# A one-core decoder layer on Trainium2: residual rows moved into the first two expert rounds, empty rounds moved to the front of the loop

## The reference

```python
x  = LayerNorm(ALPHA * x + g1 * mix)
u2 = x * (1 + sc2) + sh2
x  = LayerNorm(ALPHA * x + g2 * HierMoE(u2))   # top-1 group, then top-2 experts in that group
```

## Time and profile before

| | us |
|---|---|
| median of 3 runs | 1728.73 (1726.45 to 1728.82) |
| profiled execution, its own time | 1728.13 |
| its span, first to last instruction | 1726.0 |
| PE busy | 1568.4 (91%) |
| DVE busy | 532.8 (31%) |
| ACT busy | 203.7 (12%) |
| POOL busy | 88.4 (5%) |
| mean granted TensorE clock | 0.963 of full |

### The profile page before, as it was taken

The page is one execution under the profiler, slowest core; times in us unless marked ns, Lnnn a source line. Parts: engine busy times, 40 slices in busy tenths (PEclk is TensorE's granted clock), DMA queues, the critical chain, the costliest instruction groups (busy, mean ns, idle before and its releaser), DMA issues.

```text
span 1726.0 us, 24825 instructions
## 1 busy us (share of the span) xinstructions
PE 1568.4 (91%) x9617; PEld 896.4 (52%) x9617; DVE 532.8 (31%) x948; ACT 203.7 (12%) x343; POOL 88.4 (5%) x174
## 2 busy tenths in 40 slices
PE   3799999999999998999977999999989889899893
PEld 0256666535777754577745444444435444344351
DVE  0110029611322324422164332323223232232325
ACT  0000010200000013320043000000000000100002
POOL 3000000000111100010001000000000000000000
PEclk8799999999999899899987999999999999999997
DMA  9999988875444363454336999999999999999991
GB/s 362 422 416 400 370 316 318 324 292 209 158 135 153 132 221 121 172 207 153 137 152 243 361 419 409 415 425 424 414 400 418 399 417 415 406 424 419 418 386 61
DMA packets 79394, 537.01 MB, mean 311 GB/s; under 512 B 10385, under 2 KB 10561, under 8 KB 18065
## 3 DMA queue, kind: packets, MB, share of 16 engines
q1 hardware_dynamic: 72146, 507.62, 73.5%
q0 software_dynamic: 6576, 26.35, 4.5%
q10 hardware_dynamic: 624, 2.36, 0.3%
HBM read 533.40 MB, written 11.80 MB: 316 GB/s over the span
## 4 chain that ended last, share of the span: by engine, by line
PE 71%; DMA 17%; DVE 5%; SPq 3%; ACT 2%; issue 2%; ACTq 0%; DVEq 0%
PE ps L616 15%; PE ps L1165 14%; DMA ring<-w_gate 12%; PE ps L1008 7%; PE ps L1190 6%; PE ps L629 6%; PE ps L600 4%; PE ps L1147 3%; SPq L407 3%; DMA ring<-w_ada 3%; DMA arena<-w_in 2%; PE ps L686 2%; PE ps L662 1%; PE ps L1117 1%; DVE arena L2037 1%
## 5 line engine op out<-in xcount | busy, mean ns | idle before, releaser
L1165 PE MATMUL ps<-ring,arena 128*64 128x256 f32 x3200 | 358.8, 383 | 21.2 <-DMA ring<-w_gate 20.0
L1165 PEld LDWEIGHTS ps<-ring,arena 128*64 128x64 f32 x3200 | 227.6, 138 | 167.8 <-DMA ring<-w_gate 33.3
L616 PE MATMUL ps<-arena,ring 128*128 128x288 f32 x1024 | 256.9, 409 | 0.0
L616 PEld LDWEIGHTS ps<-arena,ring 128*128 128x128 f32 x1024 | 191.9, 190 | 69.7 <-issue 18.4
L1190 PE MATMUL ps<-arena 128*64 128x512 f32 x800 | 181.5, 601 | 20.2 <-DVE arena L2055 12.9
L600 PE MATMUL ps<-ring,silu_c 128*32 128x512 f32 x768 | 103.7, 658 | 38.0 <-POOLq L513 19.4
L1008 PE MATMUL ps<-arena,ring 128*128 128x288 f32 x512 | 124.7, 406 | 0.0
L1190 PEld LDWEIGHTS ps<-arena 128*64 128x64 f32 x800 | 54.5, 138 | 131.2 <-issue 93.0
L629 PE MATMUL ps<-ring,arena 128*128 128x512 f32 x256 | 117.0, 605 | 1.3 <-ACT arena L1263 0.7
L1147 PE MATMUL ps<-arena 64*128 64x512 f32 x384 | 104.5, 636 | 12.3 <-DVE arena L2037 10.7
L1008 PEld LDWEIGHTS ps<-arena,ring 128*128 128x128 f32 x512 | 97.2, 190 | 26.8
(11 more groups left out here) (451 smaller groups left out, 1263.0 us busy)
## 6 DMA issues: line engine op xcount, KB each, us to landing
ring<-w_gate SPq DMA_DIRECT2D x100, 1024.0 KB, 23.5
ring<-w_up SPq DMA_DIRECT2D x100, 1024.0 KB, 25.8
arena<-w_down SPq DMA_DIRECT2D x100, 1024.0 KB, 26.4
ring<-w_ada SPq DMA_DIRECT2D x96, 1024.0 KB, 10.6
ring<-w_in SPq DMA_DIRECT2D x52, 1024.0 KB, 6.5
ring<-w_o SPq DMA_DIRECT2D x16, 1024.0 KB, 6.3
ring<-cache_k SPq DMA_DIRECT2D x16, 512.0 KB, 4.4
ring<-cache_v SPq DMA_DIRECT2D x16, 512.0 KB, 4.3
```

Of the source, the lines that this page charges most:

```text
L616: last = mm(ps[:, bank, 0:T], ring[:, slot, P * t:P * (t + 1)], uT[:, t, :], start=(t == 0), stop=(t == KC - 1))
L1165: last = mm(ps[B * s:B * (s + 1), 2 + c // 4, 0:256], xgT[:, 4 * (c % 4) + t, :], ring[:, c, 512 * t + 256 * s:512 * t + 256 * (s + 1)], s ...
```

## The change

Five edits.

1. The calls 12 to 23 of `turn_tokens` are gone from ahead of the loop. Instead PE has `turn_x1` and DVE `x1_rows`: at the end of round 0 the tiles 0 and 2 (eight pieces), at the end of round 1 the tile 1 (four pieces). They go piece by piece through two PSUM banks. PE ends each of these two rounds by waiting for DVE's last piece. `acc` is zeroed by two POOL memsets first, and ALPHA times x is added to it.
2. The loops count so that empty rounds come first: `If(n + nblocks >= NBLK)`, with `i` computed in the body. PE's `turn_rows(1)` is now inside the loop.
3. The rank product stands before calls 10 and 11 of `turn_tokens`; the product for the lists follows at once, `idxs` comes before `plan`, and the experts' numbers are counted across partitions and turned by a small PE product.
4. `ln2b` is loaded by SP behind the last expert's weights, not by POOL ahead of the loop.
5. `gain_sample(0)` stands ahead of `centre(1)`; some buffers have other addresses.

```diff
@@ SP
-            with sp.Fori(1, NBLK) as i:
-                with sp.If(i < nblocks):
+            with sp.Fori(1, NBLK) as n:
+                with sp.If(n + nblocks > NBLK):
+                    i = nc.s_assert_within(sp.snap((n + nblocks + (64 - NBLK)) % 64), 0, NBLK - 1,
...
+            sp.wait_ge(tt_pe, 24)
+            sp.dma_start(ln2b, ln2.partition_broadcast(P)).then_inc(ln2_loaded, 16)
@@ POOL
             link(g.memset(xg, 0.0))
+            g.memset(acc[0], 0.0)
+            g.memset(acc[1], 0.0).then_inc(acc_clear, 1)
...
-            pool.wait_ge(tt_pe, 24)
-            pool.dma_start(ln2b, ln2.partition_broadcast(P)).then_inc(late_loaded, 16)
@@ PE
             for n in range(1, 12):
+                if n == 10:
+                    pe.wait_ge(rt_dve, 1)
...
                 turn_tokens(n, u2T)
...
-            for n in range(12, 24):
-                if n < 16:
-                    pe.wait_ge(x1_act, 4 * (n - 12) + 4)
...
-            turn_rows(1)
+            def turn_x1(first, i):
+                t0, tn = TILES[i]
+                for q in range(4):
+                    x = first + q
+                    if x >= 2:
+                        pe.wait_ge(xr_dve, x - 1)
+                    for m in range(4):
+                        last = nc.tensor.transpose(ps[0:tn, (4, 7)[x % 2], P * m:P * (m + 1)],
+                                                   rT[:, 4 * q + m, t0:t0 + tn], ident[:])
+                    last.then_inc(tt_pe, 1)
...
-            with pe.Fori(0, NBLK) as i:
-                with pe.If(i < nblocks):
+            with pe.Fori(0, NBLK) as n:
+                with pe.If(n + nblocks >= NBLK):
...
+                    with pe.If(i < 1):
+                        turn_rows(1)
...
+                    with pe.If(i < 1):
+                        pe.wait_ge(x1_act, KC)
+                        turn_x1(0, 0)
+                        turn_x1(4, 2)
+                        pe.wait_ge(xr_dve, 8)
+                    with pe.If(i > 0):
+                        with pe.If(i < 2):
+                            turn_x1(8, 1)
+                            pe.wait_ge(xr_dve, 12)
@@ DVE
+            gain_sample(0)
             for q in range(1, 4):
                 centre(q)
                 scale_rows(q)
-                gain_sample(q - 1)
-            gain_sample(3)
+                gain_sample(q)
...
-            link(v.tensor_tensor(ecmp, bc(cum[0:1, :], 1, NB1), bc(iotab[0:1, 0:NB1], 2, NE), ALU.is_le))
+            link(v.tensor_scalar(ecmp, cum, tokid[:, 0:1], None, ALU.is_le))
...
+            def x1_rows(first, i):
+                for q in range(4):
+                    x = first + q
+                    dve.wait_ge(tt_pe, 13 + x)
...
+                        v.tensor_scalar(xsrow.rearrange("t (p m) -> t m p", m=KC)[:, 4 * q:4 * q + 4, :], src,
+                                        ALPHA, None, ALU.mult).then_inc(xr_dve, 1)
...
+                        v.scalar_tensor_tensor(w, src, ALPHA, w, ALU.mult, ALU.add).then_inc(xr_dve, 1)
...
-            with dve.Fori(0, NBLK) as i:
-                with dve.If(i < nblocks):
+            with dve.Fori(0, NBLK) as n:
+                with dve.If(n + nblocks >= NBLK):
...
-            dve.wait_ge(late_loaded, 5 * 16)
+            dve.wait_ge(late_loaded, 4 * 16)
+            dve.wait_ge(ln2_loaded, 16)
```

More of the change, by code:

```diff
@@ L180, in layer @@
         xg = area(16384, D, parts=B)
[L181 to L184, removed]
+        xgT = area(18432, KC, B)
+        hid = area(19456, 256)
+        hsil = area(19712, 256)
+        hT = area(19968, 2, P)
         yout = area(13312, 1024)
@@ L580, in _ @@
                                ln2[:, 512 * q:512 * (q + 1)].partition_broadcast(32)).then_inc(late_loaded, 16)
-            with pool.Fori(0, NBLK) as i:
-                with pool.If(i < nblocks):
+            with pool.Fori(0, NBLK) as n:
+                with pool.If(n + nblocks >= NBLK):
+                    i = nc.s_assert_within(pool.snap((n + nblocks + (64 - NBLK)) % 64), 0, NBLK - 1,
+                                           skip_runtime_bounds_check_because="the branch holds it there")
                     pool.wait_ge(gathered, i * 16 + 16)
@@ L1084, in _ @@
             for n in range(1, 12):
-                turn_tokens(n, u2T)
[L1087 to L1093, removed]
-            last.then_inc(rt_pe, 1)
-            for n in range(12, 24):
-                if n < 16:
-                    pe.wait_ge(x1_act, 4 * (n - 12) + 4)
[L1098 to L1105, removed]
+                if n == 10:
+                    pe.wait_ge(rt_dve, 1)
+                    for i in range(3):
+                        mm(ps[:, 2, NE * i:NE * (i + 1)], causal[:, 0:P], both[:, i, :], start=True, stop=(i == 0))
+                        for k in range(i):
+                            mm(ps[:, 2, NE * i:NE * (i + 1)], ones[:], both[:, k, :], start=False, stop=(k == i - 1))
+                    for i in range(3):
+                        last = mm(ps[:, 3, 0:NE], ones[:], both[:, i, :], start=(i == 0), stop=(i == 2))
+                    last.then_inc(rt_pe, 1)
+                turn_tokens(n, u2T)
+            pe.wait_ge(rt_dve, 2)
+            for k in range(2):
+                for i in range(3):
+                    last = mm(ps[0:B, 4, 0:NB1], rsel[k][:, i, :], bsel[k][:, i, :],
+                              start=(k == 0 and i == 0), stop=(k == 1 and i == 2))
+            last.then_inc(rt_pe, 1)
+            pe.wait_ge(rt_dve, 3)
+            mm(ps[0:1, 5, 0:NB1], eid[0:NB1, :], ident[0:NB1, 0:NB1], start=True, stop=True).then_inc(rt_pe, 1)
             pe.sem_inc(moe_used, MOE_CHUNKS - SLOTS)
@@ L1433, in _ @@
                   ).then_inc(x1_act, 1)
[L1434 to L1441, removed]
             for nn in range(2):
@@ L1453, in _ @@
             copy_rows(1)
-            with act.Fori(0, NBLK) as i:
-                with act.If(i < nblocks):
+            with act.Fori(0, NBLK) as n:
+                with act.If(n + nblocks >= NBLK):
+                    i = nc.s_assert_within(act.snap((n + nblocks + (64 - NBLK)) % 64), 0, NBLK - 1,
+                                           skip_runtime_bounds_check_because="the branch holds it there")
                     act.wait_ge(moe_used, i * MOE_CHUNKS + (MOE_CHUNKS + 4))
@@ L2010, in _ @@
                     last.then_inc(diag_ready, 1)
-                    for x in range(20, 24):
-                        q = x % 4
-                        dve.wait_ge(tt_pe, x + 1)
-                        v.tensor_scalar(xsrow.rearrange("t (p m) -> t m p", m=KC)[:, 4 * q:4 * q + 4, :],
-                                        ps[0:TS, 6 + x % 2, :].rearrange("t (m p) -> t m p", m=4), ALPHA, None,
-                                        ALU.mult).then_inc(xr_dve, 1)
             last.then_inc(diag_ready, 1)
@@ L2044, in add_up @@
                     add_piece(n, j)
-            with dve.Fori(0, NBLK) as i:
-                with dve.If(i < nblocks):
+            with dve.Fori(0, NBLK) as n:
+                with dve.If(n + nblocks >= NBLK):
+                    i = nc.s_assert_within(dve.snap((n + nblocks + (64 - NBLK)) % 64), 0, NBLK - 1,
+                                           skip_runtime_bounds_check_because="the branch holds it there")
                     with dve.If(i > 0):
```

39 lines of the change are left out of this document (27 added, 12 removed).

## The result

The changed kernel takes 1756.7 us, the median of 4 runs (1753.84 to 1758.65), beside 1728.78 for the kernel before in as many runs (1726.45 to 1731.23). The ratio is 1.0166, with a 95% interval of 1.0141 to 1.0192. That is +28 us where +20 was forecast. The sign and the mechanism are right, the size is off. The profiled execution took 1758.4 us, 30.3 more than that of before; its span is 1756.7, which is 30.7 more.

The account below looks back on a forecast made before the run. The prediction took the pipe of 288 weight chunks to bound the kernel. Start +2.5, `ln2b` -1.1, holes +24.7 and tail -6.0 give +20.1 on 1728.1, so 1748.2, called 1748.5 as median; range 1739 to 1757 us.

Parts of the forecast that it names:

- The pipe: Expert loop: 288 weight chunks at 2.61 us each; a PE stall costs time only if it empties this pipe.
- the pipe makes it good: Rival, chance 0.07: PE's pace sets the 2.61 us, holes close over 22 rounds, about 1720 us.
- transfers catch up in the holes: Rival, chance 0.14: holes heal lag between DMA engines, each of four costing 1.5 to 2 less: 1741 us.
- The tail: Kernel's end: without empty rounds there, ACT's table load and all behind it come 6.0 us earlier.
- `ln2b` was not late: Rival at the tail, chance 0.06: the last-issued `ln2b` load makes DVE wait, adding 3 us: 1752.
- The loop starts 2.5 later: Loop start: `turn_rows(1)` at 929.4 against 926.91, behind memsets and PE's empty rounds; bounds 0.5 and 3.5 us.
- The empties: Loop start: PE's 15 empty rounds ahead of `turn_rows(1)`, 0.747 us each plus a register instruction, 12.4 us.
- Empty rounds pay for fetching code: Rival, chance 0.03: each empty round in front costs 1 us more on PE and DVE, 30 us: 1778.
- DVE's empties 9.6: Round 0: DVE's 15 empty rounds between the `where` copy and its hid product delay w_down by 9.6 us.
- Holes "24.7": Rounds 0 to 2: empty stretches of the weight pipe, 28.1 us against 3.4 before, so +24.7.
- The pause step of the sum: Ends of rounds 0 and 1: PE uses no weights for 9.3 and 5.6 us during DVE's residual pieces.
- `ln2b` away from the front, "1.1 gained": Front: not loading the 2 MB `ln2b` there frees 5.2 us of pipe, mostly empty anyway; 1.1 us gained.

Follow-up runs that it names:

- e2: The changed kernel with DVE's `where` copy moved into its loop, in round 0, so its empty rounds lie beside PE's first products: 1746.39 us.
- e3: The changed kernel with the residual's pieces at the end of rounds 7 and 8 instead of 0 and 1: 1741.92 us.
- e5: The changed kernel with the edits of e2 and e3 together, nothing else: 1734.27 us.
- e7: The changed kernel with the residual's pieces at the end of rounds 3 and 4: 1750.29 us.
- e10: As e9, with the two POOL memsets of `acc` moved behind the first gather and the `ln2s` loads: 1719.04 us.
- e4: The kernel before with only edit 2, empty rounds first on all five engines; residual, `ln2b` and routing as before: 1755.18 us.
- e9: The changed kernel with empty rounds last, loops nested 10 times 4, pieces between chunks of rounds 6 to 8, no wait at round end: 1721.44 us.

## Why the prediction was off, by its own steps

Two steps failed, both costs put too small: the start of the loop (2.5 forecast, 5.8 measured) and the two pauses for the residual's pieces (holes of 15.2 forecast behind round 0's w_down, 20.4 measured). The median lies 0.3 under the upper end of the range and two of the four runs above it; that it is inside at all is no merit of the working, since the range was drawn for other terms.

**The pipe: right.** The cost of every pause was read from whether it emptied the pipe, and e2, e3 and e5 moved the time by it. Rounds late in the loop keep their length: 31.6 us (pieces at 1457.73 and 1520.88, two rounds apart), before 31.5. The rival that the pipe makes it good fell: nothing given up in rounds 0 to 2 came back, and e7 and e3 show that only a backlog at the place of the pause covers it. Nor did transfers catch up in the holes; the landing came later than the holes explain, not earlier.

**The tail: right.** 6.0 forecast, 5.97 measured. `ln2b` was not late; DVE waited for ACT's copies.

**"The loop starts 2.5 later": mis-sized, 5.8, and outside its bounds** (0.5 to 3.5). Two terms. The memsets: I had the hold end with them at 909.1, a wait of 1.0. But the memset of xg stands behind the last store of u2 rows on POOL, and that store now waits for calls 10 and 11, which stand behind the rank product. So the memsets began at 906.52, not 903.6. DVE was held twice, 0.9 us until the first ended (L1997, 1.09 us) and 2.3 until the third did, on an instruction that takes 0.17 in e10. The Trainium skill, page SBUF — State Buffer, section Who interferes with whom, has a tensor_scalar in a 2-port mode fully blocked by a GpSimd instruction that runs; the trace agrees (2.51 against 0.17), and its TENSOR_TENSOR L2003 took 2.44 beside it. The step that failed is mine: I moved PE's calls without following them through the store to POOL's queue. With routing ahead of it 1.6 us earlier (L1997 at 907.25 for L1976 at 908.86), where 0.8 was taken, this is +1.3 at the plan. The empties: 12.4 forecast, with nothing in it for a stalled branch; they took 15 times 0.74 plus the stall of 3.3, 14.4 in all, and nothing for the added register instruction.

**"Empty rounds pay for fetching code": a rival at 0.03, partly true.** I had set it up as 1 us for each empty round. It is a price for the first skip, not for each. The Trainium skill, page Runtime: NRT & Kernel Launch, section Instruction fetch mechanics, says that a branch to code outside the fetched pages has to fetch it by DMA; two more packets and one branch of 3.3 us fit that, and 14 further branches of 0.2 us over the same body don't show such a time. My argument against the rival used empty rounds at the loop's end; there the engine had run the body just before. A skip in front has no such history. Why e4 paid 15 us for what the change paid 3.3 stays open. The body was nearly the same. What differs in the traces is the load of `ln2b` that runs beside e4's first stall, and no run here tests it.

**"DVE's empties 9.6": measured 8.05** (idle 9.83 against 1.78), at (966.1 - 958.7) / 14 = 0.53 a round: again, the register instruction adds nothing.

**Holes "24.7": measured 28.9.** The first hole, forecast 12.9, is 11.0, as DVE's empties were shorter. It is the later holes that were too small: 15.2 forecast (6.8, 5.1 and 3.3), 20.4 measured (15.1 and 5.3). The pieces were priced well, 0.98 and 0.89 each; from the end of w_down to the end of the last piece it is 8.7 us and 5.2, where 9.3 and 5.6 were forecast. What I left out is how PE comes out of a wait at a round's end. DVE's last piece ends at 987.30, the next round's first product starts at 989.26: 2.0 us in which PE passes wait, branches and round head, where before round 1 followed w_down at once. And at 988 to 992 the granted clock is 0.50, the level of 1.2 GHz, behind a stretch in which PE had done 1.7 of 4 us; the first chunk takes 3.68 where it takes 1.89 in the earlier trace rows, so the first reissue comes at 993.12, 3.9 after the round's start instead of 2.1. The pause in round 1 has both again, with 1.4 us of turnaround (1026.2 to 1027.60) and then 3.68. The pause step of the sum, then, is what failed: DVE's pieces were in it, PE's way out of the wait and the slower chunk behind it were put at nothing. They are 3.8 us in round 0, of which the cheaper pieces give 0.6 back, and 3.2 in round 1; that is about the size of the miss of 5.2, though no run separates the two. e9, which has the pieces but no wait, keeps a clock of 1.00 there and has no hole.

**`ln2b` away from the front, "1.1 gained": not seen.** If it was gained, what stays unexplained of the landing is 3 us and not 2; the cause of that is open.

The sum again with measured terms: +5.8 start, +28.9 holes, +2 unexplained, -6.0 tail, +30.7 for the span.

## What to carry to other kernels

Where a set of buffers is reloaded only as its user moves on, mark the round at which the backlog has built up, and put extra work there, spread between the pieces of the main work and with no wait at the end: the same twelve pieces left 20 us of holes in rounds 0 and 1, about 5 at the ends of rounds 7 and 8, and none inside rounds 6 to 8. An empty round of this loop took 0.53 us on DVE and 0.74 on PE; before moving such rounds, ask on each engine separately what it would wait for at their new place, and better make them few. When an instruction moves, follow it through everything that waits for it, into the queues of engines that the edit doesn't touch.

## What the runs showed of the hardware

- A skip over a long body that the engine has not run yet stalled PE for 3.3 to 3.9 us in five kernels, and in a sixth, with 2 MB of other loads in flight, the first two such skips took 5.5 and 9.7 us; later skips took 0.2 us. An empty round takes PE 0.74 us and DVE 0.53.
- A PE that waited for DVE at the end of rounds 0 and 1 lost 2.0 and 1.4 us of turnaround, then ran its next chunk at a granted clock of 0.50, 3.68 us instead of 1.89. It isn't so each time: behind round 7's wait in e3 the clock stayed at 1.00 and the chunk took 1.95.
- POOL's memsets in a row held one DVE instruction on three columns from inside the second to the end of the third: 2.51 us instead of 0.17.
